# Expert results added to x in DRAM by the scattering DMA, in place of two stored rows for each token that the last stage adds

## The chip, the cores and the metric

The kernel runs on one core of one Trainium2 chip. The metric is the device time of one execution in microseconds (us), lower is better. All data are float32.

## What is computed

One inference step of a decoder layer for 320 tokens (256 of a prompt, 64 of 8 sample sequences), each a row x of 2048 numbers. After the attention parts comes a mixture of experts, and then the final norm:

```python
eid = g_top[:, None] * EXPERTS_PER_GROUP + top_i          # two of 16 experts for each token
comb = jnp.sum(jax.nn.one_hot(eid, N_EXPERTS) * wts[..., None], axis=1)
act = jax.nn.silu(jnp.einsum('nd,edf->nef', xf, w_gate)) * jnp.einsum('nd,edf->nef', xf, w_up)
act = act * comb[..., None]
x = x + jnp.einsum('nef,efd->nd', act, w_down)             # (320, 2048)
y = rmsnorm(x, g_final)
```

So each token gets two expert results of 2048 numbers, both added to its x. That is 320 x 2 x 8 KB = 5.24 MB of results.

## The kernel before

The program is a sequence of blocks. A block has a part for each engine, and all engines meet at its end before the next block starts. Three blocks matter here, and a fourth stands between the first two.

**The late block** (lines 1533 to 1955) does the output projection, the memory attention and the norm ahead of the experts. x lies in on-chip memory as three token tiles, x[:, r, :] with r = 0, 1, 2 (128, 128 and 64 rows). When tile r is normed (semaphore `normed`), SyncE stores it to a DRAM scratch tensor `hn` (line 1563), and at the end SyncE waits for the three stores. Ahead of them in SyncE's queue stand the four loads of the first expert's gate weights (line 1560).

**The routing block** makes a table of turns from the routing. A turn is one expert with up to 64 (token, expert) pairs; with the present inputs there are 18 turns, all 16 experts are used and two of them take two turns. The table holds for each slot of a turn the token's row in `hn`, and the row of the scratch tensor `moe_y` for the result. An unused slot gets an index past the bounds, and no row is written for it.

**The expert block** (line 2121 is its end) runs the turns. In a turn TensorE multiplies the 64 gathered rows with the expert's gate and up weights (lines 2194, 2195), transposes the rows of the next turn (2184) and the activations (2202), and multiplies with the down weights (2211). SyncE loads the weights of the next turns, 12 pieces of 1 MB an expert: gate and up (line 2145) have one buffer of four pieces each and a piece is loaded when TensorE has used it, down (line 2141) has two buffers. If a turn has the same expert as the one before, nothing is loaded. ScalarE and VectorE copy the two halves of the result from PSUM to the tile y (lines 2225, 2246), and wait before it for `y_stored` of all turns before. GpSimd issues, for each turn, a gather of the next turn's rows from `hn` (line 2154) and, when y is there, two scatters of y to `moe_y` (line 2172, one for each half of y, 128 lanes of 512 numbers each, so that a token's 8 KB go as four pieces of 2 KB). It waits for the scatters of the turn before (line 2165) before it issues these. `moe_y` has 2 x 3 x 128 rows: a place for each token's first expert and another for its second, so that no piece is written twice.

**The last block** (lines 2258 on) loads g_final (line 2261), waits for all scatters (2264), loads both places for each token tile (2269: `y2[0]` over the gate weights' buffer, called W in the profile, `y2[1]` over w_u), adds both to x (2284, 2285), takes the sum of squares on ScalarE (2310), scales it (2302), takes the root (2312) and the reciprocal (2289), multiplies (2292) and stores (2273). The order on VectorE is add 0, scale 0, add 1, finish 0, scale 1, add 2, finish 1, scale 2, finish 2.

Of the kernel before, what the change touches and what calls it, by code (L numbers as in the profile page):

```python
# [69 lines left out]
def shape_constants():  # L70
# [37 lines left out]
        "pair_no": np.tile(np.arange(TURNS_MAX // 2) * 2.0, (P, 1)),  # L108
        "slot_no": np.tile(np.arange(P) % NS * 1.0, (P, 1)),
        "token1": np.stack([r * P + p + 1 for r in range(TILES) for k in range(2)], 1),  # L110
        "place1": np.stack([4 * ((k * TILES + r) * P + p) + 1 for r in range(TILES) for k in range(2)], 1),
        "lane_sum": np.where(p[:, None] % 32 == np.arange(20)[None, :], 1.0, 0.0),
        "lane": np.stack([p // NS - 1, p // NS + 1], 1),
        "page_of": np.where(p[:, None] == p[None, :] // STRIDE_ROWS, 1.0, 0.0),
# [34 lines left out]
def trunk(nc, A, out, scratch, const_at):  # L149
    top = ExitStack()  # L150
    with top:
# [1334 lines left out]
        with ExitStack() as scope:  # L1486
# [29 lines left out]
            block_loaded = [sem(f"late_block_loaded{n}") for n in range(3)]  # L1516
            first_loaded = [sem(f"late_first_loaded{q}") for q in range(4)]
            wo_loaded = [sem(f"late_wo_loaded{n}") for n in range(4)]
            x_again, wq_loaded, mk_loaded, mv_loaded, hn_stored = (sem("late_" + n) for n in (
                "x_again", "wq_loaded", "mk_loaded", "mv_loaded", "hn_stored"))  # L1520
            squared, scaled, rooted, normed, turned, drained, made, added = (sem("late_" + n) for n in (
                "squared", "scaled", "rooted", "normed", "turned", "drained", "made", "added"))
            keys_turned, keys_kept, hq_made, hq_kept, bd_zero, bd_ready, scored, max_ready, exp_ready, p_ready = (sem("m_" + n) for n in (
# [9 lines left out]
            with nc.Block() as block:  # L1533
                @block.sync
                def _(sp):
                    w_out = w_view("w_out")
                    for q in range(4):
                        sp.dma_start(w_blocks[0][:, 4 * q:4 * q + 4, :], w_out[:, 4 * q:4 * q + 4, 0:512]).then_inc(first_loaded[q], 16)
                    sp.dma_start(x[:, 0:2, :], A["x_prompt"][0].rearrange("(r p) n -> p r n", p=P)).then_inc(x_again, 16)
                    sp.dma_start(x[0:NS, 2, :], A["x_sample"].rearrange("b t n -> (b t) n")).then_inc(x_again, 16)  # L1540
                    sp.dma_start(w_blocks[1], w_out[:, :, 512:1024]).then_inc(block_loaded[0], 16)
                    for b in range(NB):
                        sp.dma_start(m_k[:, b], tiled("cache_mem_k", b)).then_inc(mk_loaded, 16)
                    sp.dma_start(w_r[:, :, 0:4], w_view("w_router_group")).then_inc(wr_loaded, 16)
                    sp.dma_start(w_r[:, :, 4:20], w_view("w_router_expert")).then_inc(wr_loaded, 16)
                    for n in range(2, 4):
                        sp.wait_ge(made, 3 * (n - 1))
                        sp.dma_start(w_blocks[n], w_out[:, :, 512 * n:512 * n + 512]).then_inc(block_loaded[n - 1], 16)
                    sp.wait_ge(made, 9)
                    sp.dma_start(w_q, w_view("w_mem_q")).then_inc(wq_loaded, 16)  # L1550
                    sp.wait_ge(keys_turned, 16)
                    for b in range(NB):
                        sp.dma_start(m_v[:, b], tiled("cache_mem_v", b)).then_inc(mv_loaded, 16)
                    sp.wait_ge(hq_made, MH)
                    for n in range(4):
                        sp.dma_start(w_o[:, :, 512 * n:512 * n + 512],
                                     A["w_mem_o"][0].rearrange("(c p) n -> p c n", p=P)[:, :, 512 * n:512 * n + 512]).then_inc(wo_loaded[n], 16)
                    sp.wait_ge(o_made, 3)
                    for dst, src, loaded in gate_loads(0):
                        sp.dma_start(dst, src).then_inc(loaded, 16)  # L1560
                    for r in range(TILES):
                        sp.wait_ge(normed, 2 * TILES + r + 1)
                        sp.dma_start(scratch["hn"][r * P:r * P + ROWS[r]], hn_of(MOE, r)).then_inc(hn_stored, 16)
                    sp.wait_ge(hn_stored, 16 * TILES)

                @block.gpsimd
                def _(pool):
# [531 lines left out]
        with ExitStack() as scope:  # L2099
# [21 lines left out]
            with nc.Block() as block:  # L2121
# [26 lines left out]
                def _(pool):  # L2148
# [7 lines left out]
                                                bounds_check=SEQ + NS - 1, oob_is_err=False).then_inc(gathered[u], 16)  # L2156

                    gather(0, 0)
                    y_rows = scratch["moe_y"].rearrange("r (n c) -> (r n) c", c=512)

                    def step(turn, u, i):

# [7 lines left out]
                        pool.sem_inc(pool_passed, 1)  # L2170
                        for h in range(2):
                            pool.indirect_dma_start(out=y_rows, out_offset=bass.IndirectOffsetOnAxis(ap=to_row[:, u, h:h + 1], axis=0),  # L2172
                                                    in_=y[:, u, h, :], in_offset=None, bounds_check=8 * TILES * P - 1, oob_is_err=False).then_inc(y_stored, 16)
                    turns(pool, step)
                    pool.wait_ge(gathered[0], 16)

# [71 lines left out]


        with ExitStack() as scope:  # L2250
            y2 = [w[:, :, :].rearrange("p (r c) f -> p r (c f)", r=4) for w in (w_g, w_u)]
            gf = y2[0][:, 3, :]
            junk = w_d[:, 0, 0, :]
            ms = sb(scope, "f_ms", [P, TILES])
            gf_loaded, summed, squared, scaled, rooted, ready, stored = (sem("f_" + n) for n in (
                "gf_loaded", "summed", "squared", "scaled", "rooted", "ready", "stored"))
            y_loaded = [sem(f"f_y_loaded{r}") for r in range(TILES)]
            with nc.Block() as block:
                @block.sync
                def _(sp):  # L2260
# [3 lines left out]
                    sp.wait_ge(y_stored, n * 64)  # L2264
                    for r in range(TILES):
                        rows = P if r < 2 else NS
                        for k in range(2):
                            a = (k * TILES + r) * P
                            sp.dma_start(y2[k][0:rows, r, :], scratch["moe_y"][a:a + rows]).then_inc(y_loaded[r], 16)  # L2269
                    for r in range(TILES):  # L2270
                        sp.wait_ge(ready, r + 1)
                        dst = out["y_p"][0, r * P:(r + 1) * P] if r < 2 else out["y_s"].rearrange("b t n -> (b t) n")
# [5 lines left out]
                def _(dve):  # L2278
                    own = dve_steps.on(dve)

                    def add(r):
                        rows = P if r < 2 else NS
                        dve.wait_ge(y_loaded[r], 32)
                        own.link(dve.tensor_tensor(x[0:rows, r, :], x[0:rows, r, :], y2[0][0:rows, r, :], ALU.add))  # L2284
                        dve.tensor_tensor(x[0:rows, r, :], x[0:rows, r, :], y2[1][0:rows, r, :], ALU.add).then_inc(summed, 1)  # L2285

                    def finish(r):
                        dve.wait_ge(rooted, r + 1)
# [3 lines left out]
                        dve.scalar_tensor_tensor(out=x[:, r, :], in0=x[:, r, :], scalar=ms[:, r:r + 1], in1=gf,  # L2292
                                                 op0=ALU.mult, op1=ALU.mult).then_inc(ready, 1)

                    for r in range(TILES + 1):
                        if r < TILES:
                            add(r)
                        if r >= 1:
                            finish(r - 1)
                        if r < TILES:  # L2300
                            dve.wait_ge(squared, r + 1)
                            dve.tensor_scalar(ms[:, r:r + 1], ms[:, r:r + 1], 1.0 / D, EPS, ALU.mult, ALU.add).then_inc(scaled, 1)  # L2302

                @block.scalar
                def _(act):
                    for r in range(TILES):
                        act.wait_ge(summed, r + 1)
                        if r:
                            act.wait_ge(squared, r)
                        act.activation(junk, x[:, r, :], ACT.Square, accum_out=ms[:, r:r + 1]).then_inc(squared, 1)  # L2310
                        act.wait_ge(scaled, r + 1)
                        act.activation(ms[:, r:r + 1], ms[:, r:r + 1], ACT.Sqrt).then_inc(rooted, 1)  # L2312
# [28 lines left out]
```

## Time and profile before

| | us |
|---|---|
| median of 3 runs | 1881.65 (1880.87 to 1887.93) |
| the profiled execution | 1877.32 |
| span of its trace | 1875.5 |
| span from the trace's 1829 to its end (last scatters, last block) | 46.5 |

The span runs from the first to the last event of the trace. The profiled execution took 1.8 us more than its span. Times in the trace are microseconds from the span's start. "PEclk" is the granted clock of TensorE as a share of full speed (1.0 is 2.4 GHz, 0.5 is 1.2 GHz), and "DMA share" is the mean busy share of the core's 16 DMA engines (it can read 1.01 or 1.02, since packets overlap slightly). Queue q1 carries the DMAs of SyncE, q0 those of GpSimd.

### The profile page before, as it was taken

Reading aid. Unit: us, or ns where it says so; the run is one execution under the profiler, and the core shown is the slowest. Engines: PE = TensorE matmul, PEld = TensorE weight load, DVE = VectorE, ACT = ScalarE, POOL = GpSimd, SP = SyncE. Lnnn points to the kernel's source line nnn. Section 1 sums busy time; section 2 is a strip of 40 time slices with the busy share of each in tenths; the row PEclk is TensorE's granted clock in tenths of the full one; section 3 lists DMA queues with packets and bytes.
Section 4 is the critical chain, followed back from the end, with each engine's and each line's share of the span. In section 5 each row is a group of like instructions: output and inputs, shape, how many; then the busy total and the mean of one; then the engine's idle time right before and its main releaser. Section 6 shows DMA issues by size and latency. Waiting matters only on the chain. (4 is left out here: it accounts for less than half of the span.)

```text
span 1875.5 us, 17915 instructions
## 1 busy us (share of the span) xinstructions
PE 1564.6 (83%) x6791; PEld 811.9 (43%) x6791; DVE 388.8 (21%) x765; ACT 293.0 (16%) x620; POOL 74.3 (4%) x107
## 2 busy tenths in 40 slices
PE   7999999987999378886769999967978878798880
PEld 4444445555556355563344456543323332233230
DVE  3101100001222343336541021351101010011014
ACT  3000000111222022225520002310000000000001
POOL 0000000000000000000000000000110101010100
PEclk9999999997999589996869999977998989899895
DMA  8463332423310054410057222468998999999955
GB/s 317 182 271 127 135 114 90 153 90 137 120 66 6 23 170 144 147 59 8 1 180 250 90 90 91 167 259 308 395 406 310 398 407 403 395 353 413 408 231 194
DMA packets 113799, 380.15 MB, mean 203 GB/s; under 512 B 17459, under 2 KB 55387, under 8 KB 83047
## 3 DMA queue, kind: packets, MB, share of 16 engines
q1 hardware_dynamic: 108050, 343.27, 48.7%
q0 software_dynamic: 5552, 27.89, 4.3%
q10 hardware_dynamic: 144, 8.26, 1.0%
q8 instruction: 36, 0.59, 0.1%
q14 instruction: 17, 0.14, 0.0%
HBM read 390.41 MB, written 26.49 MB: 222 GB/s over the span
## 5 line engine op out<-in xcount | busy, mean ns | idle before, releaser
L2194 PE MATMUL bank<-W,hT_e 128*64 128x512 f32 x576 | 277.6, 635 | 59.5 <-DMA w_u<-in_w_exp_up 58.6
L2195 PE MATMUL bank<-w_u,hT_e 128*64 128x512 f32 x576 | 277.6, 635 | 0.0
L2194 PEld LDWEIGHTS bank<-W,hT_e 128*64 128x64 f32 x576 | 81.4, 146 | 248.5 <-issue 161.8
L2211 PE MATMUL bank<-W,actT 128*64 128x512 f32 x576 | 143.9, 657 | 9.0 <-ACT actT L2222 9.0
L719 PE MATMUL bank<-subT,w 128*128 128x504 f32 (+1 forms) x320 | 134.5, 550 | 0.0
L519 PE MATMUL bank<-raw,hT 128*128 128x512 f32 (+1 forms) x320 | 131.6, 573 | 0.6 <-PEq L280 0.6
L519 PE MATMUL bank<-w_in,hT 128*128 128x512 f32 (+2 forms) x320 | 123.7, 547 | 0.0
L1588 PE MATMUL bank<-W,mixT 128*128 128x512 f32 x256 | 114.0, 606 | 1.6 <-DVE mixT L1809 1.6
L519 PEld LDWEIGHTS bank<-raw,hT 128*128 128x128 f32 x320 | 61.5, 193 | 67.8 <-issue 67.6
L519 PEld LDWEIGHTS bank<-w_in,hT 128*128 128x128 f32 x320 | 60.4, 190 | 61.1 <-issue 61.1
L2211 PEld LDWEIGHTS bank<-W,actT 128*64 128x64 f32 x576 | 44.0, 150 | 95.6 <-issue 90.2
L2240 DVE SCALAR_TENSOR_TENSOR act_w<-bank,row_w,gate 64x512 f32<-64x512 f32 x18 | 13.6, 757 | 334.0 <-ACT gate L2220 334.0
L2195 PEld LDWEIGHTS bank<-w_u,hT_e 128*64 128x64 f32 x576 | 81.4, 146 | 0.0
L1588 PEld LDWEIGHTS bank<-W,mixT 128*128 128x128 f32 x256 | 49.3, 194 | 63.8 <-issue 61.7
L719 PEld LDWEIGHTS bank<-subT,w 128*128 128x128 f32 x320 | 55.9, 207 | 33.1 <-issue 32.4
L2220 ACT ACTIVATE gate<-bank 64x512 f32<-64x512 f32 x18 | 10.6, 589 | 322.2 <-PE bank L2195 322.2
L708 PEld LDWEIGHTS bank<-const,rawg 128*128 128x128 f32 (+1 forms) x320 | 38.4, 145 | 44.6 <-issue 35.3
L708 PE MATMUL bank<-const,rawg 128*128 128x128 f32 (+1 forms) x320 | 45.8, 269 | 8.3 <-ACT rawg L769 8.3
L2172 POOL DMA_INDIRECT scratch_moe_y<-y,to_row x36 | 36.2, 1006 | 406.7 <-DVE y L2246 401.2
L1049 PE MATMUL bank<-v_in,pT 128*128 128x256 f32 x192 | 45.6, 387 | 7.2 <-ACT pT L1087 7.2
L999 PE MATMUL bank<-const,k_in 128*128 128x128 f32 x192 | 31.8, 312 | 22.6 <-DMA k_in<-in_cache_win_k 18.2
L2184 PE MATMUL bank<-const,rows_in 64*128 64x64 f32 x304 | 37.5, 277 | 15.1 <-DMA rows_in<-scratch_hn,from_row 15.1
(364 smaller groups left out, 1669.6 us busy)
## 6 DMA issues: line engine op xcount, KB each, us to landing
W<-in_w_exp_down SPq DMA_DIRECT2D x76, 1024.0 KB, 23.8
W<-in_w_exp_gate SPq DMA_DIRECT2D x72, 1024.0 KB
w_u<-in_w_exp_up SPq DMA_DIRECT2D x72, 1024.0 KB
raw<-in_w_in SPq DMA_DIRECT2D x3, 4096.0 KB
W<-in_w_out SPq DMA_DIRECT2D x3, 4096.0 KB, 13.5
w_in<-in_w_in SPq DMA_DIRECT2D x2, 4096.0 KB, 14.7
k_in<-in_cache_sel_k SPq DMA_DIRECT2D x64, 128.0 KB, 2.2
v_in<-in_cache_sel_v SPq DMA_DIRECT2D x64, 128.0 KB, 2.4
```

The lines of the kernel that those rows point to most:

```text
L519: mm = pe.matmul(bank[4 * u + r][:, 0:width], hT[:, c, r * P:(r + 1) * P], w, start=(c == 0), stop=(c == KC - 1))
L708: mm = pe.transpose(bank[q % 4][:, g * n:g * n + n], rawg[0:n, q // 4, a:a + P], ident[0:n, 0:n])
L719: mm = pe.matmul(bank[4 + u][:, 0:heads * nk], w1[:, u, 8 * r + q, :], x[:, :, r:r + nk], start=(q == 0 and r == 0), stop=(q == 7 and r == 1))
L999: mm = pe.transpose(bank[4 + n % 2][:, k * P:k * P + P], k_in[:, 4 * m + k, c * P:c * P + P], ident)
L1049: mm = pe.matmul(bank[3][:, 256:256 + KVW], p, v, start=(n == 0), stop=(n == len(terms) - 1))
L1588: mm = pe.matmul(to, hT[:, c, r * P:r * P + P], w(c, slice(0, 512)), start=(c == 0), stop=(c == chunks - 1))
L2172: pool.indirect_dma_start(out=y_rows, out_offset=bass.IndirectOffsetOnAxis(ap=to_row[:, u, h:h + 1], axis=0), in_=y[:, u, h, :], in_offset ...
L2184: mm = pe.transpose(bank[6 + h][:, k * NS:k * NS + NS], rows_in[:, u, 8 * h + k:D:KC], ident[0:NS, 0:NS])
L2194: pe.matmul(bank[4 + u][0:NS, :], hT[:, u, c, :], w_g[:, c, :], start=(c == 0), stop=(c == KC - 1))
L2195: mm = pe.matmul(bank[4 + u][UP, :], hT[:, u, c, :], w_u[:, c, :], start=(c == 0), stop=(c == KC - 1))
L2211: mm = pe.matmul(bank[2 * u + n // 2][lane, :], actT[:, q, :], w_d[:, u, q, 512 * n:512 * n + 512], start=(q == 0), stop=(q == 3))
L2240: dve.scalar_tensor_tensor(out=act_w[UP, :], in0=bank[4 + u][UP, :], scalar=row_w[UP, bass.ds(turn, 1)], in1=gate[UP, :], op0=ALU.mult, op ...
```

## The change

x is now stored to `moe_y` in the late block (line 1564), tile by tile behind the tile of `hn`. The scatters add what they carry to the row that is there (`compute_op=ALU.add`), and both experts of a token have the same place. The last block then loads one tensor of 3 tiles straight into x, and has no additions; the sum of squares waits for the load alone. The order on VectorE is scale r, finish r for each tile.

```diff
-        "place1": np.stack([4 * ((k * TILES + r) * P + p) + 1 for r in range(TILES) for k in range(2)], 1),
+        "place1": np.stack([4 * (r * P + p) + 1 for r in range(TILES) for k in range(2)], 1),
...
                         sp.dma_start(scratch["hn"][r * P:r * P + ROWS[r]], hn_of(MOE, r)).then_inc(hn_stored, 16)
+                        sp.dma_start(scratch["moe_y"][r * P:r * P + ROWS[r]], x[0:ROWS[r], r, :]).then_inc(x_stored, 16)
                     sp.wait_ge(hn_stored, 16 * TILES)
+                    sp.wait_ge(x_stored, 16 * TILES)
...
-                                                    in_=y[:, u, h, :], in_offset=None, bounds_check=8 * TILES * P - 1, oob_is_err=False).then_inc(y_stored, 16)
+                                                    in_=y[:, u, h, :], in_offset=None, bounds_check=4 * TILES * P - 1, oob_is_err=False, compute_op=ALU.add).then_inc(y_stored, 16)
...
-                        for k in range(2):
-                            a = (k * TILES + r) * P
-                            sp.dma_start(y2[k][0:rows, r, :], scratch["moe_y"][a:a + rows]).then_inc(y_loaded[r], 16)
+                        sp.dma_start(x[0:rows, r, :], scratch["moe_y"][r * P:r * P + rows]).then_inc(x_loaded[r], 16)
...
-                    def add(r):
-                        rows = P if r < 2 else NS
-                        dve.wait_ge(y_loaded[r], 32)
-                        own.link(dve.tensor_tensor(x[0:rows, r, :], x[0:rows, r, :], y2[0][0:rows, r, :], ALU.add))
-                        dve.tensor_tensor(x[0:rows, r, :], x[0:rows, r, :], y2[1][0:rows, r, :], ALU.add).then_inc(summed, 1)
+                    def mean(r):
+                        dve.wait_ge(squared, r + 1)
+                        dve.tensor_scalar(ms[:, r:r + 1], ms[:, r:r + 1], 1.0 / D, EPS, ALU.mult, ALU.add).then_inc(scaled, 1)
...
-                        act.wait_ge(summed, r + 1)
+                        act.wait_ge(x_loaded[r], 16)
```

On SyncE, at the end of the late block (`scratch_hn` and `scratch_moe_y` are the DRAM tensors, W holds the normed rows), before:

```order
L1560 DMA W<-in_w_exp_gate 128x2048 x4
L1563 DMA scratch_hn<-W 128x2048 x2
L1563 DMA scratch_hn<-W 64x2048
L1533 UNCONDITIONAL_BRANCH
L1958 UNCONDITIONAL_BRANCH
L1962 DMA w_u<-in_w_exp_up 128x2048 x4
```

and in the changed kernel:

```order
L1560 DMA W<-in_w_exp_gate 128x2048 x4
L1563 DMA scratch_hn<-W 128x2048
L1564 DMA scratch_moe_y<-x 128x2048
L1563 DMA scratch_hn<-W 128x2048
L1564 DMA scratch_moe_y<-x 128x2048
L1563 DMA scratch_hn<-W 64x2048
L1564 DMA scratch_moe_y<-x 64x2048
L1533 UNCONDITIONAL_BRANCH
```

Three stores have come in, each behind its tile of `hn`, and the last of them is the last DMA of the block.

On VectorE, the last block before:

```order
L2284 TENSOR_TENSOR x<-x,W 128x2048
L2285 TENSOR_TENSOR x<-x,w_u 128x2048
L2302 TENSOR_SCALAR f_ms<-f_ms 128x1
L2284 TENSOR_TENSOR x<-x,W 128x2048
L2285 TENSOR_TENSOR x<-x,w_u 128x2048
L2289 RECIPROCAL f_ms<-f_ms 128x1
L2292 SCALAR_TENSOR_TENSOR x<-x,f_ms,W 128x2048
L2302 TENSOR_SCALAR f_ms<-f_ms 128x1
L2284 TENSOR_TENSOR x<-x,W 64x2048
L2285 TENSOR_TENSOR x<-x,w_u 64x2048
L2289 RECIPROCAL f_ms<-f_ms 128x1
L2292 SCALAR_TENSOR_TENSOR x<-x,f_ms,W 128x2048
```

(a scale, a reciprocal and a product for tile 2 follow), and in the changed kernel the whole of it:

```order
L2282 TENSOR_SCALAR f_ms<-f_ms 128x1
L2286 RECIPROCAL f_ms<-f_ms 128x1
L2289 SCALAR_TENSOR_TENSOR x<-x,f_ms,W 128x2048
L2282 TENSOR_SCALAR f_ms<-f_ms 128x1
L2286 RECIPROCAL f_ms<-f_ms 128x1
L2289 SCALAR_TENSOR_TENSOR x<-x,f_ms,W 128x2048
L2282 TENSOR_SCALAR f_ms<-f_ms 128x1
L2286 RECIPROCAL f_ms<-f_ms 128x1
L2289 SCALAR_TENSOR_TENSOR x<-x,f_ms,W 128x2048
```

The six additions are gone, and no tile's chain stands behind another tile's addition. TensorE's program and the order on ScalarE and GpSimd are the same in both kernels.

## Rows read from the trace of the kernel before

**Rows 1.** The page: busy time of the engines over the span.
```profile
PE 1564.6 (83%) x6791; PEld 811.9 (43%) x6791; DVE 388.8 (21%) x765; ACT 293.0 (16%) x620; POOL 74.3 (4%) x107
```

**Rows 2.** Windows of the expert stage: length, busy times (instructions), PEclk, DMA share, GB/s.
```profile
1290.00:1420.00 130.00, 111.25 (x505) 41.02 (x502) 11.04 (x16) 8.77 (x15) 13.51 (x20) 0.93 1.01 402
1420.00:1429.00 9.00, 8.04 (x34) 3.98 (x36) 2.04 (x3) 0.95 (x2) 0.00 (x0) 0.65 0.21 73
1429.00:1643.00 214.00, 178.58 (x797) 65.42 (x794) 19.05 (x28) 14.31 (x23) 23.61 (x35) 0.92 1.01 396
...
1648.00:1807.00 159.00, 138.16 (x638) 51.07 (x636) 14.39 (x21) 12.18 (x19) 20.05 (x29) 0.95 1.01 405
1807.00:1829.00 22.00, 18.13 (x84) 6.92 (x80) 2.74 (x4) 1.55 (x3) 0.18 (x1) 0.92 0.05 19
```

**Rows 3.** DMA queues, 1310:1836: packets, MB, share of 16 engines' time.
```profile
q1 hardware_dynamic: 25340, 184.49, 87.4%
q0 software_dynamic: 4240, 10.07, 6.1%
```

**Rows 4.** DMA queues, 1440:1444, a full turn's scatter.
```profile
q0 software_dynamic: 167, 0.59, 36.2%
```

**Rows 5.** Line 2172, the scatter: its waits, who waited, issue to landing.
```profile
  DVE y L2246: 401.2, 18
...
DMA to landing us min/median/max: 2.3/6.8/8.3
```

**Rows 6.** The last scatter's landing, and GpSimd at the block's end.
```profile
1830.61 0.99 POOL L2172 DMA_INDIRECT scratch_moe_y<-y,to_row  x1 [0.30 <-issue]
...
DMA to landing us min/median/max: 2.3/2.3/2.3
...
L2121 POOLq DRAIN  x1: 6281/6281/6281, 1829.9 to 1829.9; - x1
```

**Rows 7.** Line 673, an earlier block's end; line 248 in 528:528.5, its last gather.
```profile
L673 POOLq DRAIN  x1: 8925/8925/8925, 527.8 to 527.8; - x1
...
DMA to landing us min/median/max: 8.4/8.4/8.4
```

**Rows 8.** Line 1563 in 1237:1238 (issue at 1237.4), line 1533, the block's end.
```profile
DMA to landing us min/median/max: 4.2/4.2/4.2
...
L1533 DVEq DRAIN  x1: 458/458/458, 1242.8 to 1242.8; - x1
```

**Rows 9.** Timeline of the last stage: start, us, instruction, idle before.
```profile
1836.40 0.34 SPq L2261 DMA_DIRECT2D W<-in_g_final  x1
1837.45 0.33 SPq L2269 DMA_DIRECT2D W<-scratch_moe_y  x1
...
1853.78 1.28 ACT L2312 ACT_TABLE_LOAD   x1
...
1870.88 0.52 SPq L2273 DMA_DIRECT2D out_y_s<-x  x1
```

**Rows 10.** Line 2269 in 1837.4:1837.6, the first token tile's load.
```profile
DMA to landing us min/median/max: 7.2/7.2/7.2
```

**Rows 11.** The chain that ended last: start, us, what.
```profile
1837.83 9.26 DMA w_u<-scratch_moe_y
...
1849.43 2.30 DVE x L2285
...
1851.76 2.01 ACT W L2310 x2
...
1853.80 0.15 DVE f_ms L2302
...
1868.06 0.21 ACT f_ms L2312
...
1868.30 0.17 DVE f_ms L2289
...
1868.50 2.35 DVE x L2292
```

More of the change, by code:

```diff
@@ L1518, in trunk @@
             wo_loaded = [sem(f"late_wo_loaded{n}") for n in range(4)]
-            x_again, wq_loaded, mk_loaded, mv_loaded, hn_stored = (sem("late_" + n) for n in (
-                "x_again", "wq_loaded", "mk_loaded", "mv_loaded", "hn_stored"))
+            x_again, wq_loaded, mk_loaded, mv_loaded, hn_stored, x_stored = (sem("late_" + n) for n in (
+                "x_again", "wq_loaded", "mk_loaded", "mv_loaded", "hn_stored", "x_stored"))
             squared, scaled, rooted, normed, turned, drained, made, added = (sem("late_" + n) for n in (
@@ L2158, in _ @@
                     gather(0, 0)
-                    y_rows = scratch["moe_y"].rearrange("r (n c) -> (r n) c", c=512)
+                    y_rows = scratch["moe_y"].rearrange("r (n c) -> (r n) c", c=512)[0:4 * TILES * P]
                     def step(turn, u, i):
@@ L2250, in trunk @@
         with ExitStack() as scope:
-            y2 = [w[:, :, :].rearrange("p (r c) f -> p r (c f)", r=4) for w in (w_g, w_u)]
-            gf = y2[0][:, 3, :]
+            gf = w_g[:, 0:4, :].rearrange("p c f -> p (c f)")
             junk = w_d[:, 0, 0, :]
             ms = sb(scope, "f_ms", [P, TILES])
-            gf_loaded, summed, squared, scaled, rooted, ready, stored = (sem("f_" + n) for n in (
-                "gf_loaded", "summed", "squared", "scaled", "rooted", "ready", "stored"))
-            y_loaded = [sem(f"f_y_loaded{r}") for r in range(TILES)]
+            gf_loaded, squared, scaled, rooted, ready, stored = (sem("f_" + n) for n in (
+                "gf_loaded", "squared", "scaled", "rooted", "ready", "stored"))
+            x_loaded = [sem(f"f_x_loaded{r}") for r in range(TILES)]
             with nc.Block() as block:
@@ L2293, in finish @@
                                                  op0=ALU.mult, op1=ALU.mult).then_inc(ready, 1)
[L2295 to L2302, printed above, removed]
+                    for r in range(TILES):
+                        mean(r)
+                        finish(r)
                 @block.scalar
```

## The prediction, made before the changed kernel was run

> **What bounds the kernel now.** The page calls TensorE the busiest engine, 83% of the span [rows 1]. That mixes stages, so I read the windows of the stage that the change touches. Outside its two pauses the expert stage, 1290 to 1807, has a DMA share of 1.01 at 396 to 405 GB/s: three windows, 130 + 214 + 159 = 503 us, in which the 16 DMA engines never rest [rows 2]. TensorE is busy for about 85% of them and has slack. In the pauses (one of them is the window with a share of 0.21; the other is 5 us at 1643) a turn has the expert of the turn before, nothing is loaded and TensorE sets the pace; so too from 1807 to 1829, behind the last weights [rows 2]. So in 503 us of this stage each microsecond of DMA engine time that an edit adds or takes away is one of the kernel. Then I read the queues, which tell what the scatters and gathers of GpSimd take: q0 moved 10.07 MB in 6.1% of 526 us, 32.1 us of all 16 engines, and q1 (nearly all weights) had 87.4% [rows 3]. Last comes the chain that ended last: from 1837 on nothing but the last block's loads, additions and norms [rows 9, 11].
>
> **Term 1, the last block.** Before, the first tile's two loads have landed at 1837.83 + 9.26 = 1847.09, and the last product ends at 1868.50 + 2.35 = 1870.85 [rows 11]; the store issued at 1870.88 ends the span at 1875.5 [rows 9]. After, the first load stands where W's load stood, behind g_final alone; that one was issued at 1837.45 and took 7.2 us [rows 9, 10], so x0 is there at 1844.65. Squares 2.01, then scale 0.15 [rows 11] with ScalarE's table load of 1.28 beside it [rows 9] (before, VectorE's additions for tile 1 covered that load; now it is bare and hides the scale), root 0.21, reciprocal 0.17, product 2.35 [rows 11]: 6.0, with 0.02 to 0.05 of handover at each step 6.15, so tile 0 ends at 1850.8. Tile 1 lands about 2.4 us behind tile 0, when the second load did before (1847.09), and ScalarE, free at 1848.2, has its squares by 1850.2, beneath tile 0's product. What is left a tile is scale 0.15, root 0.21, reciprocal 0.17, product 2.35 and handovers, 3.0. Two such: 1856.8. The store then takes the same 4.6 us, so the end is 1861.4: **-14.1 us**. If the loads come 1 us earlier or later than this, so does the end: -15 to -13. The six additions of about 2.3 us [rows 11] are 14 us of work too, but a part of them lay beside other steps, and what goes for certain is the chain above.
>
> **Term 2, three stores of x in the late block.** Those of tiles 0 and 1 are issued 8 us and more ahead of the last one and lie beneath the work for the later tiles. The last is issued 0.5 us behind hn's, at 1237.9. Hn's, of the same size, landed 4.2 us after its issue at 1237.4, while VectorE's last work ended the block at 1242.8 + 0.46 = 1243.3 [rows 8]. So hn's landed at 1241.6 with 1.7 us to spare. X's lands 0.5 us later if it doesn't wait for hn's bytes, at 1242.1 (cost 0), and at 1243.4 to 1244 if it does. The cover is VectorE's copies; past them every engine waits, since the block's end is shared. I take **+0.3**, bounds 0 and 1.
>
> **Term 3, the adding scatter.** The carried bytes stay 5.24 MB. The nearest row is the plain scatter itself: in 1440:1444, which holds a full turn's scatter, q0 moved 0.59 MB in 36.2% of 4 us, 1.45 us, thus 2.46 us for 1 MB, and 12.9 us for all scatters [rows 4]. An addition has to read its destination too, 5.24 MB that no row here shows. Lower bound: the read runs beside the write and costs nothing. I see no gain, since nothing of the plain scatter goes away. Next: the read takes the engines as long as the carried bytes do, +12.9. Next: it is as dear as the gathers, which have the other 32.1 - 12.9 = 19.2 us for 10.07 - 5.24 = 4.83 MB [rows 3], so +20.8. Still higher: source read, destination read and write stand in one row, each at the plain price, +25.8. Upper bound: nothing is pipelined, and each engine waits the 2.3 us of a lone scatter's landing [rows 6] for each of some 80 packets of 4 KB (5.24 MB / 4 KB / 16), +184. I take the row nearest to it in size of piece and place, the scatter's own, +12.9, of which the last two turns' scatters fall beyond 1800 into open time; 95% counts: **+12.3**. What the Trainium skill says of an adding DMA ("Collectives: The Full Stack", the section on the bandwidth ceiling) is that the addition itself costs nothing but needs two source reads, so that the engine moves half as much in a time; that would make it +12.9 before the 95% as well, but it also speaks against the change, for a read that is hidden would leave the whole 14 us as gain.
>
> Behind the scatter two things wait. The gather of the next turn is issued right behind it in the same queue. And GpSimd, ScalarE and VectorE wait for `y_stored` one turn later; a scatter lands in 6.8 us at the median and 8.3 at most, and GpSimd then waits 401.2 us in 18 turns, 22 us a turn, for the next y [rows 5]. A scatter twice as long is hidden there; one of over 25 us is not.
>
> **Term 4, the last scatter.** It was issued at 1830.61 and landed in 2.3, but GpSimd's drain at the block's end lasted until 1829.9 + 6.3 = 1836.2 and released the last block [rows 6]. In an earlier block a drain from 527.8 to 536.7 ended where a gather issued at 528.0 landed (8.4) [rows 7]. So I read the drain as one that waits for the DMA, and a longer last scatter is on the path. It holds few pieces; doubled, and with one read of DRAM more, **+1**. If the 3.3 us between landing and drain's end are cover, 0; if the landing doubles, 2.3.
>
> **Sum.** 1877.32 (the profiled execution) - 14.1 + 0.3 + 12.3 + 1 = 1876.8, a change of -0.5. The median of the runs shown is 4.3 us above the profiled execution, so the forecast for the median is 1881.65 - 0.5, about **1881**. What this measurement can tell from no change is about 0.5%, 9.4 us.
>
> **Rivals.**
> A: the destination read is hidden, or nearly (term 3 under 3 us). For it: reads and writes are different work, and the plain scatter's own read and write overlap. Against it: a DMA engine here moves some 25 GB/s whatever it does (405 / 16 in the windows [rows 2]; 0.59 MB in 1.45 us is 407 GB/s too [rows 4]), so its time goes by bytes passed through. Result: -14.1 + 0.3 + 0 to 3 + 0.5, -13 to -10, 1868.5 to 1871.5.
> B, the other side: the adding scatter is dearer than a second read, since the engine waits for the destination's bytes before it can write. From 25.8 (three passes in a row) up: it is slower by over 9.4 us as soon as the scatters' added engine time is above 23.4 us / 0.95, about 24 us or 2.9 times the plain total. At +25.8 to +45 the result is +11 to +29, 1893 to 1911. For it: gathers already cost 1.6 times as much a byte as scatters, for no reason that the rows tell. Against it: other packets fill the engine between. Full serialization, +184 and 2060, would be its extreme; the Trainium skill ("DMA: Bandwidth & Descriptors", on two DMAs through the same engine) tells of two adding packets of one row where the second read stale data when it followed directly. By that rule adding packets overlap, and this extreme falls away; no run here shows it. I leave 4 in 100 for it.
> C: the gather is late behind the longer scatter. It is issued 2 us behind it, its rows are needed when the next gate and up products end. TensorE then waits, but in the saturated windows it has slack of some 15%; only in the two pauses and at the end does it count: +1 to +5 on top of the sum, 1882 to 1886. This is no other sign, only a part of the range.
> D: the change does less than it says: the last block is held not by additions but by its loads. The loads halve as well, so this moves term 1 by 1 or 2 us at most.
>
> **How the numbers follow.** A 0.24; the forecast (with C and D), term 3 from 3 to 24, 0.46; B 0.30, with its extreme. The same cases give faster 0.25, same 0.45, slower 0.30. Likeliest case's own range: 1872 to 1891. For the whole: down to 1868, the low end of A, and up to 1904, the middle of B (+35 of engine time); this leaves about 0.05 below and 0.14 above.
>
> **What the profile will show.** Term 1: the last block's first square 7 us after the load's issue, the last product 12 us after the first load's landing. Term 3: q0's share of 526 us goes from 6.1% to about 8.6% and the window from the first turn to the last weights is 12 us longer, at a DMA share of 1.01 still. Rival A: share and length as before. B: q0 over 11%, GB/s well under 396. C: TensorE's waits for the gathered rows grow. The prediction is wrong above all if the time of one adding packet isn't twice that of a plain one.

## The result, and the profile after

| | before | after |
|---|---|---|
| median, us | 1881.74 (18 runs, 1870.1 to 1887.93) | 1890.6 (18 runs, 1882.33 to 1900.49) |
| ratio to before | | 1.005 (1.0031 to 1.007) |
| the same comparison, repeated later | | 1.0025 (0.9996 to 1.0053) |
| span of the profiled execution | 1875.5 | 1890.5 |

The changed kernel is slower by 0.25 to 0.5%, where 0.5 us less was forecast; the first interval lies wholly above 1, the second just reaches it. The range, 1868 to 1904, holds the time.

Since the two spans differ by 15.0 us and the medians by 8.9, the first reading is where the two traces part. The ends of blocks show it. In the rows for line 1533 (end of the late block) and line 2121 (end of the expert block) of the trace of before, the GpSimd event is the last to arrive and its time is the release of the next block:

```profile
L1533 POOLq EVENT_SEMAPHORE  x2: 17/17/17, 1243.3 to 1243.3; - x2
...
L2121 POOLq EVENT_SEMAPHORE  x2: 17/17/17, 1836.2 to 1836.3; - x2
```

The changed kernel, the late block's end (who came last) and the expert block's end, line 2123 there:

```profile
L1533 POOLq EVENT_SEMAPHORE  x2: 17/17/17, 1255.4 to 1255.5; - x2
...
L1533 DVEq DRAIN  x1: 456/456/456, 1253.7 to 1253.7; - x1
L1533 SPq COMPARE_BRANCH  x1: 38/38/38, 1255.2 to 1255.2; - x1
```

```profile
L2123 POOLq EVENT_SEMAPHORE  x2: 17/17/17, 1865.7 to 1865.8; - x2
...
L2123 POOLq DRAIN  x1: 7406/7406/7406, 1858.3 to 1858.3; - x1
```

Late block's end: 1243.3 before, 1255.5 after, 12.2 us later. Only 1.2 us of that are the change's. Before, VectorE was done at 1242.8 + 0.46 = 1243.3 [rows 8] and the release came at once. After, it was done at 1254.2, but SyncE came out of its wait for the stores at 1255.2 and the release at 1255.5, 1.3 us behind VectorE. The other 11 us were there when the block began, in stages that both kernels have alike. The end of the block ahead of it (line 1409), before and then after:

```profile
L1409 POOLq EVENT_SEMAPHORE  x2: 17/17/17, 961.0 to 961.1; - x2
...
L1409 POOLq EVENT_SEMAPHORE  x2: 17/17/17, 971.9 to 971.9; - x2
```

Those 11 us go with TensorE's granted clock: its mean over the twelve windows of 100 us from 0 to 1200, between its two levels of 1.2 and 2.4 GHz, was 0.927 in the trace of before and 0.912 in this one.

From the late block's end to the last block's start: 593.0 before, 610.3 after, **+17.3**. Last block: 39.2 before, 24.7 after, **-14.5**. So the change itself makes 1.2 + 17.3 - 14.5 = +4.0 in this pair of traces.

The expert stage in windows (length, busy time of PE, PEld, DVE, ACT, POOL, then PEclk, DMA share, GB/s), as in [rows 2]:

```profile
1302.00:1436.00 134.00, 114.22 (x511) 42.02 (x506) 11.98 (x17) 9.34 (x15) 18.11 (x20) 0.87 1.01 387
...
1445.00:1664.00 219.00, 178.18 (x781) 64.49 (x777) 18.34 (x26) 14.30 (x23) 31.58 (x35) 0.85 1.02 383
...
1670.00:1833.00 163.00, 141.51 (x638) 51.74 (x634) 14.75 (x21) 12.17 (x19) 26.89 (x29) 0.90 1.00 392
1833.00:1856.00 23.00, 18.43 (x84) 7.12 (x84) 2.04 (x3) 0.96 (x2) 0.18 (x1) 0.93 0.11 45
```

The DMA engines are saturated as before, in 134 + 219 + 163 = 516 us, 13 more than the 503 of before, at 383 to 392 GB/s in place of 396 to 405 [rows 2]. The granted clock in them is lower too, 0.85 to 0.90 in place of 0.92 to 0.95, but the clock doesn't set this stage's time: from the late block's end to the last block it was 0.89 in experiment 4 (603.4 us) and in experiment 9 (588.7 us), and 0.86 in experiment 3 (594.6 us). The queues from 1323 to 1866 say what makes it longer (packets, MB, share), as [rows 3]; then 1456:1460, behind the issue of a full turn's scatters, as [rows 4]:

```profile
q1 hardware_dynamic: 25366, 184.61, 85.4%
q0 software_dynamic: 6544, 10.07, 8.9%
```

```profile
q0 software_dynamic: 175, 0.33, 44.4%
```

q0 carries the same 10.07 MB, but takes 8.9% of 543 us, 48.3 us of all engines, where it had taken 32.1: **+16.2 us**. The weights on q1 take more as well, 85.4% of 543 us against 87.4% of 526, 463.7 us against 459.7 for the same bytes to 0.1 MB: **+4.0 us**, which no run explains; over the whole stage of both pairs of traces it is 3.1 to 4.0. In the second window 1.78 us of engine time go with 0.33 MB, 5.4 us for 1 MB in place of 2.46 [rows 4], 2.2 times as much. That ratio is rough, since both windows also hold a part of the gather that was issued behind the scatters (1438.7 before, 1455.1 after). The packets rose from 4240 to 6544 [rows 3]: an adding scatter's lanes are no longer put together two to a packet (the working is in the last section).

The scatter's own row, its waits and its landing, as [rows 5]:

```profile
L2174 POOL DMA_INDIRECT scratch_moe_y<-y,to_row x36: 1559/1567/1609, 1327.3 to 1859.6; - x36
...
  DVE y L2248: 349.6, 18
...
DMA to landing us min/median/max: 3.6/9.4/12.1
```

It lands in 9.4 us at the median, not 6.8. GpSimd waits 124.0 us for the scatters of the turn before (`y_stored`; 75.5 before), but then still 349.6 us for y, so the first wait costs nothing. But TensorE waits for the gathers queued behind it, first before, then after:

```profile
  DMA rows_in<-scratch_hn,from_row: 15.1, 5
```

```profile
  DMA rows_in<-scratch_hn,from_row: 65.0, 15
```

The last block (timeline, as [rows 9]):

```profile
1865.94 0.34 SPq L2262 DMA_DIRECT2D W<-in_g_final  x1
...
1874.02 1.91 ACT L2302 ACTIVATE W<-x 128x2048 f32<-128x2048 f32 x1 [17.36 <-DMA x<-scratch_moe_y]
...
1876.04 1.28 ACT L2304 ACT_TABLE_LOAD   x1
...
1877.77 2.35 DVE L2289 SCALAR_TENSOR_TENSOR x<-x,f_ms,W 128x2048 f32<-128x2048 f32 x1
...
1880.65 2.35 DVE L2289 SCALAR_TENSOR_TENSOR x<-x,f_ms,W 128x2048 f32<-128x2048 f32 x1
...
1883.54 2.35 DVE L2289 SCALAR_TENSOR_TENSOR x<-x,f_ms,W 128x2048 f32<-128x2048 f32 x1
1885.91 0.51 SPq L2272 DMA_DIRECT2D out_y_s<-x  x1
```

The load lands at 1874.0, squares, table load, and three products end at 1885.9; 12 us after the load, as worked out.

### The profile page after: what moved, and what is told of

Its sections match the earlier page's. It is cut to its first block and busy times, and to the rows that moved or that the text cites. A ratio compares the mean times of both kernels' runs of the same rounds, so it can differ in the third digit from the quotient of the medians.

```text
span 1890.5 us, 17910 instructions
## 1 busy us (share of the span) xinstructions
PE 1585.3 (84%) x6791; PEld 821.5 (43%) x6791; DVE 376.2 (20%) x759; ACT 292.9 (15%) x620; POOL 94.9 (5%) x107
## 5 line engine op out<-in xcount | busy, mean ns | idle before, releaser
L2196 PE MATMUL bank<-W,hT_e 128*64 128x512 f32 x576 | 257.9, 604 | 24.2 <-DMA w_u<-in_w_exp_up 23.4
L2197 PE MATMUL bank<-w_u,hT_e 128*64 128x512 f32 x576 | 257.9, 604 | 0.0
L2213 PE MATMUL bank<-W,actT 128*64 128x512 f32 x576 | 169.7, 755 | 9.0 <-ACT actT L2224 9.0
L2213 PEld LDWEIGHTS bank<-W,actT 128*64 128x64 f32 x576 | 49.6, 173 | 116.5 <-issue 110.7
L2174 POOL DMA_INDIRECT scratch_moe_y<-y,to_row x36 | 56.3, 1565 | 355.1 <-DVE y L2248 349.6
L2186 PEld LDWEIGHTS bank<-const,rows_in 64*128 64x128 f32 x304 | 35.1, 201 | 80.3 <-issue 80.3
L1012 PE MATMUL bank<-keyT,q_now 128*128 128x512 f32 x96 | 45.0, 619 | 8.2 <-DVE keyT L1059 6.5
```

What stands on the lines that cost most here:

```text
L1012: pe.matmul(bank[n], q_now[:, c, :], keyT[:, c, 512 * n:512 * n + 512], start=(c == 0), stop=(c == 1))
L2186: mm = pe.transpose(bank[6 + h][:, k * NS:k * NS + NS], rows_in[:, u, 8 * h + k:D:KC], ident[0:NS, 0:NS])
L2196: pe.matmul(bank[4 + u][0:NS, :], hT[:, u, c, :], w_g[:, c, :], start=(c == 0), stop=(c == KC - 1))
L2197: mm = pe.matmul(bank[4 + u][UP, :], hT[:, u, c, :], w_u[:, c, :], start=(c == 0), stop=(c == KC - 1))
L2213: mm = pe.matmul(bank[2 * u + n // 2][lane, :], actT[:, q, :], w_d[:, u, q, 512 * n:512 * n + 512], start=(q == 0), stop=(q == 3))
```

## Experiments

The stages of all traces are compared by the ends of blocks, read as above. "Expert" runs from the late block's end to the last block's start, "last" from there to the span's end. Before and the changed kernel have two traces each, whose expert stages differ by 3.1 and 0.1 us; every other kernel has one.

| kernel | expert, us | last, us | ratio to before |
|---|---|---|---|
| before | 593.0 | 39.2 | |
| before, again | 589.9 | 39.2 | 0.9994 (0.9973 to 1.0016) |
| changed | 610.3 | 24.7 | 1.005 (1.0031 to 1.007) |
| changed, again | 610.4 | 24.9 | 1.0025 (0.9996 to 1.0053) |
| changed, plain scatter | 588.3 | 25.0 | 0.9942 (0.9916 to 0.9967) |
| before, adding scatter | 607.5 | 39.6 | 1.0139 (1.0112 to 1.0166) |
| before, x stored | 594.6 | 38.3 | 1.0029 (1.0012 to 1.0046) |
| before, twice the plain scatters | 612.1 | 39.6 | 1.0096 (1.0064 to 1.0129) |
| changed, early gather | 603.4 | 25.1 | 1.0021 (0.9996 to 1.0045) |
| before, early gather | 586.0 | 40.2 | 0.9965 (0.9936 to 0.9993) |
| before, early gather and new last block | 588.7 | 35.2 | 0.9979 (0.9952 to 1.0005) |
| the same with GpSimd adding | 588.8 | 37.3 | 0.9976 (0.995 to 1.0003) |
| changed, early gather, g_final later | 606.8 | 23.4 | 1.001 (0.9986 to 1.0035) |

**1. The changed kernel with a plain scatter.**

```diff
-  in_=y[:, u, h, :], in_offset=None, bounds_check=4 * TILES * P - 1, oob_is_err=False, compute_op=ALU.add)
+  in_=y[:, u, h, :], in_offset=None, bounds_check=4 * TILES * P - 1, oob_is_err=False)
```

> The changed kernel with the addition taken out of the scatter and nothing else: x is still stored, both results of a token go to the same place, the last block still loads one row for each token. It leaves out the additions, so y comes from whichever result of a token was written last. Theory S (engine time: an adding packet holds a saturated DMA engine 2.3 times as long as a plain one, 16 us more over all scatters, and the saturated windows pass it on): q0 falls back to 6.1% of the stage, the stage from the late block's end to the last block shrinks by about 17 us, and the kernel is about 13 us faster than before (ratio 0.993), some 20 us faster than the changed one. Rival Q (the stores of x or something else in the changed kernel cost the time, the addition little): within 5 us of the changed kernel, ratio 1.002 to 1.005.

Measured: 0.9942 (0.9916 to 0.9967). Its trace, queue q0 from 1311 to 1840 and the two ends of blocks:

```profile
q0 software_dynamic: 4240, 10.07, 6.1%
...
L1533 POOLq EVENT_SEMAPHORE  x2: 17/17/17, 1246.2 to 1246.3; - x2
...
L2123 POOLq EVENT_SEMAPHORE  x2: 17/17/17, 1834.6 to 1834.6; - x2
...
L2123 POOLq DRAIN  x1: 6289/6289/6289, 1828.2 to 1828.2; - x1
```

q0 is back at 6.1%, the expert stage at 588.3 us, 22.0 less than in the changed kernel, with the last block as short as there. So the addition alone, the one word taken out, costs the stage 22 us in this pair (14.5 to 22 over all traces with the late gather), and without it, in a kernel that leaves out the sums, the change would have gained 0.6%. Rival Q falls.

**2. The kernel before with an adding scatter.**

```diff
+                    for k in range(2):
+                        a = k * TILES * P
+                        sp.dma_start(scratch["moe_y"][a:a + 2 * P], A["x_prompt"][0]).then_inc(y_set, 16)
+                        sp.dma_start(scratch["moe_y"][a + 2 * P:a + 2 * P + NS], A["x_sample"].rearrange("b t n -> (b t) n")).then_inc(y_set, 16)
...
-  bounds_check=8 * TILES * P - 1, oob_is_err=False)
+  bounds_check=8 * TILES * P - 1, oob_is_err=False, compute_op=ALU.add)
```

> The kernel before with the addition put into the scatter and nothing else of the change: two places for each token, the last block adds both. So that there is something to add to, both places are filled in the late block with the step's input x by four DMAs from DRAM to DRAM, 5.2 MB in all, beside work that TensorE bounds; y is then of x plus the results plus twice the input. Theory S: the expert block is 17 us longer than before, the last block as before, the kernel 15 to 20 us slower (ratio 1.008 to 1.011). Rival Q: no slower than 5 us (ratio below 1.003).

Measured: 1.0139 (1.0112 to 1.0166, five runs), more than either theory gave. The expert stage is 607.5 us, 14.5 to 17.6 more than in the two traces of before, as theory S has it, and the last block 0.4 longer. That is 1.0096 at most; the rest of the 26 us, 8 or more, lies outside the stages that the change touches and no trace here shows what it is. The DMAs from DRAM to DRAM, which stand ahead of the late block's loads of the router and of later weights, are one candidate, not tried by themselves.

**3. The kernel before with the stores of x alone.**

```diff
                         sp.dma_start(scratch["hn"][r * P:r * P + ROWS[r]], hn_of(MOE, r)).then_inc(hn_stored, 16)
+                        sp.dma_start(scratch["x_copy"][r * P:r * P + ROWS[r]], x[0:ROWS[r], r, :]).then_inc(x_stored, 16)
                     sp.wait_ge(hn_stored, 16 * TILES)
+                    sp.wait_ge(x_stored, 16 * TILES)
```

> The kernel before with the three stores of x behind those of hn and the wait for them, to a scratch tensor that nobody reads; the output is the reference's. The trace of the changed kernel shows SyncE 1.2 us behind VectorE at the late block's end. Theory S: +1 us in time, not to be told from nothing (ratio 1.000 to 1.001), and 1 to 1.5 us at that block's end in the trace. Rival Q: 3 us or more, some of it outside that block (ratio over 1.002).

Measured: 1.0029 (1.0012 to 1.0046), above what theory S gave and where rival Q has it. The late block's end in its trace (the release, TensorE, VectorE, SyncE):

```profile
L1533 POOLq EVENT_SEMAPHORE  x2: 17/17/17, 1257.4 to 1257.4; - x2
...
L1533 PEldq DRAIN  x1: 747/747/747, 1254.8 to 1254.8; - x1
L1533 DVEq DRAIN  x1: 458/458/458, 1255.6 to 1255.6; - x1
L1533 SPq COMPARE_BRANCH  x1: 38/38/38, 1257.2 to 1257.2; - x1
```

VectorE is done at 1256.1, SyncE at 1257.2, and the release comes at 1257.4, 1.3 us behind VectorE, as in the changed kernel. That the stores cost 1.2 us at this place is shown; the 1 to 7 us that the interval has beyond it are not explained by any row found, so rival Q isn't refuted in the medians.

**4. The early gather in the changed kernel.**

```diff
                     gather(0, 0)
+                    gather(1, 1)
...
-                        pool.wait_ge(h_turned, turn * 2)
-                        gather(turn + 1, 1 - u)
+                        pool.wait_ge(h_turned, turn * 2 + 2)
+                        gather(turn + 2, u)
```

> The changed kernel with each gather issued one turn earlier: the gather for turn t + 2 ahead of the scatters of turn t in GpSimd's queue, not behind them (the buffer is free by then). Work and DMA bytes are the same. In the changed kernel TensorE waited 65.0 us for gathered rows, 15.1 before. Theory S: these waits go (a few us are left at the first turn), but in the saturated windows the DMA engines set the pace, so only the 2 to 4 us in the pauses and behind the last weights come back: ratio to before 1.001 to 1.004. Rival G (the late gather is what costs, by holding TensorE and with it the release of weight buffers and the granted clock): 10 us or more come back, ratio below 1.000.

Measured: 1.0021 (0.9996 to 1.0045). TensorE's waits for gathered rows in its trace, and the ends of blocks:

```profile
  DMA rows_in<-scratch_hn,from_row: 11.4, 1
...
L1533 POOLq EVENT_SEMAPHORE  x2: 17/17/17, 1244.4 to 1244.5; - x2
...
L2123 POOLq EVENT_SEMAPHORE  x2: 17/17/17, 1847.8 to 1847.9; - x2
```

The waits fall from 65.0 us to 11.4, all of it in the first turn. The stage loses 6.9 us of 610.3, more than the 2 to 4 of theory S. So of 54 us of TensorE's waiting, 47 had been slack under the DMA engines: its waits for the up weights rise from 23.4 to 66.7 us. Rival G, 10 us or more, falls in the trace: 10 to 14 us of excess stay (603.4 against 589.9 to 593.0), and against the kernel before with the same early gather (experiment 7) it is the whole 17.4.

**5. Before against itself.** Nothing is edited.

> The kernel before, unchanged, timed against itself and profiled a second time. In the medians the changed kernel is 8.9 us slower, but between its trace and that of before the three stages that the change touches differ by 4.0 us only (1.2 in the late block, 17.4 from there to the last block, -14.6 in the last block); 11 us lie in stages ahead of the change. Theory S: these 11 us, and some of the rest, are what one execution differs from the next by, so the ratio is 1.000 within 0.25% and this trace's early stages lie anywhere from 962 to 973 us. Rival L (every program built differently carries a few us of its own): this copy, identical, stays at 1.000 with early stages at 962, while each altered kernel lies above.

Measured: 0.9994 (0.9973 to 1.0016). Ends of blocks:

```profile
L1533 POOLq EVENT_SEMAPHORE  x2: 17/17/17, 1248.9 to 1248.9; - x2
...
L2121 POOLq EVENT_SEMAPHORE  x2: 17/17/17, 1838.8 to 1838.8; - x2
```

The late block's end is at 1248.9, 5.6 us later than in the first trace, with nothing changed; it was at 1237.1 in the earliest trace of an altered kernel (the one with the new last block) and at 1257.4 in the latest (x stored). Apart from the stores' 1.2 us that spread of 20 us goes with no edit, and it is why the stages are compared one by one. It goes with the granted clock: the mean over the twelve windows of 100 us from 0 to 1200 was 0.933 in the earliest, 0.927 and 0.920 in the two traces of before, and 0.912 and 0.913 in the two latest (changed, 1255.5, and x stored). Rival L's sign, early stages that stay at 962 in an identical copy, did not come: the block ahead of the late one ends at 966.7 here, and at 961.1 in experiment 4, an altered kernel.

**6. The changed kernel again.** Nothing is edited.

> The changed kernel, unchanged, a second trace and more runs. Theory S: ratio 1.003 to 1.007 again, q0 at some 8.9% of the stage, 15 to 19 us more than before from the late block's end to the last block, about 14.5 us less in the last block. Rival: the stage's excess in the first trace was an accident of that execution (under 12 us here).

Measured: 1.0025 (0.9996 to 1.0053). Ends of blocks and GpSimd's drain:

```profile
L1533 POOLq EVENT_SEMAPHORE  x2: 17/17/17, 1247.2 to 1247.3; - x2
...
L2123 POOLq EVENT_SEMAPHORE  x2: 17/17/17, 1857.6 to 1857.7; - x2
...
L2123 POOLq DRAIN  x1: 7406/7406/7406, 1850.1 to 1850.1; - x1
```

The expert stage is 610.4 us (the first trace gave 610.3), the last block 24.9, so the first trace's excess was no accident. With the means of two traces each the change makes +1.2, +18.9 (610.35 against 591.45) and -14.4 (24.8 against 39.2): **+5.7 us**, a ratio of 1.003, at the lower edge of the first interval and inside the second.

**7. The early gather in the kernel before.** The edit is that of experiment 4.

> The kernel before with each gather issued one turn earlier, the gather for turn t + 2 ahead of the scatters of turn t; the output is the reference's. TensorE waited 15.1 us for gathered rows in the trace of before, 11.2 of it for the first turn's. Theory S: at most 4 us come back, ratio 0.998 to 1.001. Rival G (the gather's place in the queue was worth 5 us and more to the changed kernel for reasons that hold before as well): ratio under 0.997.

Measured: 0.9965 (0.9936 to 0.9993); the stage is 586.0 us, 3.9 to 7.0 less than in the traces of before, though only about 4 us of waits went away. The ratio is the one of rival G here, and its interval reaches into theory S's: more comes back than the waits explain, and about as much as in the changed kernel. The gather's place in the queue is worth some 3 to 7 us with either scatter. With the early gather the adding scatters still cost 17.3 us (603.4 and 606.8 in experiments 4 and 11 against 586.0, 588.7 and 588.8 in 7, 9 and 10), so at most 1 or 2 us of their 18.9 are the gather's.

**8. Twice the plain scatters.**

```diff
-                        for h in range(2):
-                            pool.indirect_dma_start(out=y_rows,
+                        for h, y_rows in ((0, y_rows_a), (1, y_rows_a), (0, y_rows_b), (1, y_rows_b)):
+                            pool.indirect_dma_start(out=y_rows,
```

> The kernel before with every plain scatter followed by a second plain one of the same rows to another scratch tensor that nobody reads. It adds to q0 what a plain scatter costs, 12.7 us of the 16 engines over all turns, with no addition and no read of the destination, and 2.6 us a turn on GpSimd. Theory S (the addition costs by the engine time that it takes, no more): this kernel is slower by 12 to 17 us (ratio 1.006 to 1.009), since 12.7 us pass through and the gather behind the scatters is later still. Rival R (the addition stalls the engines beyond the time its packets show, so plain scatters are cheaper than their share): under 6 us (ratio below 1.003).

Measured: 1.0096 (1.0064 to 1.0129, six runs), just above theory S. The queues from 1316 to 1861, the ends of blocks and the drain:

```profile
q1 hardware_dynamic: 25317, 184.33, 84.8%
q0 software_dynamic: 7120, 15.32, 8.6%
...
L1533 POOLq EVENT_SEMAPHORE  x2: 17/17/17, 1248.9 to 1249.0; - x2
...
L2121 POOLq EVENT_SEMAPHORE  x2: 17/17/17, 1861.0 to 1861.1; - x2
...
L2121 POOLq DRAIN  x1: 10764/10764/10764, 1850.2 to 1850.2; - x1
```

The stage is 612.1 us, 20.6 above the mean of before. The drain at its end is 10.8 us, 4.5 above that of before [rows 6], so 16.1 us lie in the turns. Here nothing is added, and a plain load of the queue of about the size of the addition's (q0 took 8.6% of 545 us, 46.9 against 32.1) costs what the addition costs: +16.1 for +14.8 of engine time here, +17.8 (18.9 less 1.1 of drain) for +16.2 there. Rival R falls. It is the engine time, at 1.1 for each us of q0. With what the weights' own packets take more (q1: 84.8% of 545 us, 462.2, +2.5 here; +4.0 there) 17.3 us of engine time gave 16.1 here and 20.2 gave 17.8 there: about nine tenths pass.

This run also prices a plain scatter by itself: 14.8 us for all 36, not the 12.9 that the window of [rows 4] gave. An adding one then takes 14.8 + 16.2 = 31.0, 2.1 times as much.

**9. Plain scatters, early gather and a new last block.**

```diff
-                    sp.dma_start(gf, A["g_final"].partition_broadcast(P)).then_inc(gf_loaded, 16)
...
+                        if r == 0:
+                            sp.dma_start(gf, A["g_final"].partition_broadcast(P)).then_inc(gf_loaded, 16)
...
-                        dve.wait_ge(y_loaded[r], 32)
+                        dve.wait_ge(y_loaded[2 * r], 16)
                         own.link(dve.tensor_tensor(x[0:rows, r, :], x[0:rows, r, :], y2[0][0:rows, r, :], ALU.add))
+                        dve.wait_ge(y_loaded[2 * r + 1], 16)
```

> The kernel before with the early gather, and a last block without an adding DMA: g_final is loaded behind the first token tile, and VectorE starts the first addition as soon as the first of the two places has landed. The output is the reference's. From the trace of before: the first place lands 2.4 us ahead of the second and another 2.4 us earlier without g_final (1 MB) ahead of it, and VectorE, busy for nearly all of the 23.7 us behind, follows. Last block 34 to 36 us in place of 39.1 (changed kernel 24.6), the expert stage some 586 as with the early gather before: ratio 0.993 to 0.996.

Measured: 0.9979 (0.9952 to 1.0005). The last block is 35.2 us, as expected; the stage is 588.7, 2.7 more than in experiment 7, and the ratio is higher than the 0.993 to 0.996 expected. Of the kernels that compute the reference these plain-scatter ones are the fastest, by 0.2 to 0.35%; between 7 and 9 the intervals don't decide.

**10. The same, with GpSimd making one addition.**

```diff
+                    pool.wait_ge(y_loaded[4], 16)
+                    pool.tensor_tensor(x[0:NS, 2, :], x[0:NS, 2, :], y2[0][0:NS, 2, :], ALU.add).then_inc(half_summed, 1)
```

> As the run with the new last block, and GpSimd makes the first addition of the third token tile (64 rows), which takes one 2.3 us addition off VectorE. If GpSimd is no slower than 5 us at it and doesn't slow VectorE: last block 2 us shorter, ratio 0.001 lower. If the two engines hinder each other, the same or longer.

Measured: 0.9976 (0.995 to 1.0003). GpSimd's addition, and VectorE's behind it:

```profile
1857.94 6.60 POOL L2313 TENSOR_TENSOR x<-x,W 64x2048 f32<-64x2048 f32 x1 [23.25 <-DMA W<-scratch_moe_y]
...
1864.57 2.28 DVE L2291 TENSOR_TENSOR x<-x,w_u 64x2048 f32<-64x2048 f32 x1 [4.32 <-POOL x L2313]
```

It takes 6.60 us where VectorE takes 2.3, more than the 5 us up to which a gain was expected, and VectorE idles 4.3 us for it. The last block is 2.1 us longer, not shorter.

**11. The adding scatter at its best.** The early gather of experiment 4 and g_final behind the first tile, as in 9.

> The changed kernel with the early gather and with g_final loaded behind the first token tile: the adding scatter at its best. The output is the reference's. The last block starts its squares 2.4 us earlier: 22.5 us in place of 25, expert stage some 603 us as with the early gather. Ratio 0.999 to 1.002, and 8 to 12 us slower than the plain scatters with the new last block. Rival: within 3 us of them, if the last block's gain outweighs the 17 us of the adding scatters.

Measured: 1.001 (0.9986 to 1.0035). The last block is 23.4 us, 11.8 less than with plain scatters at their best (9), and the stage 606.8, 18.1 more. The stores' 1.2 us come on top, so the adding version loses by 7.5 us in the traces and 7.5 in the medians (1883.82 against 1876.27), a little under the 8 to 12 expected. The rival, within 3 us, falls.

## Why the prediction was wrong

Term by term, against the means of two traces each:

- **Term 1, the last block**: -14.1 forecast, -14.4 measured. The chain ran as worked out, with ScalarE's table load bare.
- **Term 2, the stores of x**: +0.3 forecast, +1.2 measured, and the same in the kernel with the stores alone. The failed part is that I put the price between 0 and 1, near the case in which x's last store doesn't wait for hn's bytes. It was issued 0.6 us behind hn's last one and took 6.2 us where that one took 4.2, so it landed at 1255.2, past VectorE's end at 1254.2:

```profile
DMA to landing us min/median/max: 6.2/6.2/6.2
```

- **Term 3, the adding scatter**: +12.3 forecast, +17.8 measured. This is the step that failed and turned the sign. The mechanism holds: engine time of a saturated DMA passes to the kernel (experiments 1, 2 and 8). Its size was wrong: 12.9 us of added engine time stood in the sum, and 20.2 were measured. First, the plain scatters' price was read too low: the window 1440:1444 that gave 12.9 also holds a part of the gather issued at 1438.7, and twice the scatters gave 14.8. Second, the addition multiplies that by 2.1 and not by 2, which together make +16.2. Third, the weights' packets take 4.0 us more beside the longer scatters, a term that the sum put at nothing. The share that passes, 95% in the sum, came out near that, 17.8 of 20.2 or 88%. The gather's lateness (rival C) is in the 17.8 with 1 or 2 us.
- **Term 4, the last scatter**: +1 forecast. GpSimd's drain went from 6.28 [rows 6] to 7.41 us, +1.1. That the drain waits for the DMA is supported by twice the scatters (10.8).

The sum of the four as measured is +5.7 in place of -0.5. The forecast of "about no change" came from two terms of 14 and 12 us that nearly cancel, so an error of 40% in the unknown one was the whole result; that it was close was luck of two like terms, and no sign that the price was known. The text's bound, slower by 9.4 us from about 24 us of added engine time on, takes the 95% twice: by its own terms it is 9.4 + 14.1 - 0.3 - 1 = 22.2, over 0.95, 23.4 us. Beyond that slip it was not tested: by the same sum q0's 16.2 us would have given +2.6, and the touched stages show +5.7. Rival A was ruled out (q0's time did not stay), so was B (its sign was a q0 share of over 11%, and it is 8.9%). The argument against A, that a DMA engine moves 25 GB/s whatever it does, doesn't fit the prediction's own rows: the gathers moved 4.83 MB in 19.2 us, 16 GB/s an engine. Rival C happened in its mechanism, waits for gathers of 65.0 us in place of 15.1, and experiment 4 prices its removal at 6.9 us; but the kernel before gets 3.9 to 7.0 back by the same edit, so what C adds to the change is 1 or 2 us (experiment 7). D did not happen.

The Trainium skill's account of an adding DMA, told of a ReduceScatter ("Collectives: The Full Stack", the section on the bandwidth ceiling), is two source reads and so half the rate. The 2.1 times of these runs lie a little above it. The extreme of rival B, adding packets that don't overlap (+184 us), did not come, as the section on two DMAs through the same engine in "DMA: Bandwidth & Descriptors" suggests.

What stays open: the medians of the changed kernel exceed those of before by 8.9 us in one comparison and by about 5 in the other, and experiments 2 and 3 lie 8 to 10 and some 4 us above what the stages that they touch account for in their traces. The stages ahead differ between traces with the granted clock, as experiment 5 tells; why one execution is granted less than another isn't known, and whether an altered program carries a few us of its own there is not settled. Before against itself showed none in the median. Open too is why the weights' packets take longer beside the adding scatters.

## What to carry to other kernels

An adding DMA isn't free of charge beside a plain one: here it took 2.1 times the engine time. It should pay where the DMA engines have time to spare, which no run here tried; this kernel's scatters sit in a stage where they have none. Moving work from a stage that an engine's chain bounds (14 us of it) into one where DMA time is the bound has to be priced at nearly 1 us for each us of engine time that all queues together take more, here 1.1 us for each us of the scatters' own. And when a forecast is a small difference of two large terms, the unshown one decides its sign: take its bounds for the chances, not its middle.

## What the runs showed of the hardware that was not expected

- An adding scatter's 2 KB lanes go one to a packet, a plain one's two. Doubling the 36 plain scatters adds 7120 - 4240 = 2880 packets to q0, which is 36 x (64 + 16); the addition adds 6544 - 4240 = 2304, which is 36 x 64, for the same 10.07 MB. With 128 lanes a scatter this is 64 packets for the lanes when plain and 128 when adding, beside 16 others. And GpSimd takes 1.57 us to issue one, 1.01 for a plain one.
- GpSimd needs 6.60 us for an addition of 64 x 2048 float32 numbers, VectorE 2.28 us.
- The HBM line of the page doesn't show the destination reads of the adding DMA. Before, then after:

```profile
HBM read 390.41 MB, written 26.49 MB: 222 GB/s over the span
...
HBM read 387.79 MB, written 29.11 MB: 221 GB/s over the span
```

The read bytes fall by the 2.62 MB that the last block no longer loads, while 5.24 MB of destinations had to be read; the written bytes grow by the 2.62 MB of x.
